# Building the expert gate matrix: one float32 matmul per token against three bfloat16 ones on one-hots made four tokens at a time

## The chip, the cores and the metric

The kernel runs on one core of one Trainium2 chip. The metric is the device time of the whole program in microseconds (us), median of three runs. TensorE (PE) multiplies, VectorE (DVE) and ScalarE (ACT) do elementwise work, GpSimd (POOL) one subtraction that is repeated, and SyncE (SP) issues the transfers.

## The reference

The program is one layer of a decoder trunk over 512 tokens of width 1024: a combined input projection, two attention mixers, and then a feed-forward of retrieved single-neuron experts. The change is in this last part alone, in float32:

```python
def peer_ffn(xn, w_query, sub_keys, u, v):          # per block of 128 tokens
    q = (xb @ w_query).reshape(BLOCK, PEER_HEADS, 2, PEER_HALF)
    s = jnp.einsum('thcd,hckd->thck', q, sub_keys)
    s1, i1 = lax.top_k(s[:, :, 0], PEER_TOPK)       # 16 of 128 keys, twice, in 8 heads
    s2, i2 = lax.top_k(s[:, :, 1], PEER_TOPK)
    cand_s = s1[..., :, None] + s2[..., None, :]
    cand_i = i1[..., :, None] * N_KEYS + i2[..., None, :]
    ...
    top_s, top_c = lax.top_k(cand_s, PEER_TOPK)     # 16 experts (i, j) of 128 x 128 per head
    g = jax.nn.softmax(top_s, axis=-1)
    act = jax.nn.gelu(jnp.einsum('thkd,td->thk', ue, xb), approximate=False)
    return jnp.einsum('thk,thkd->td', g * act, ve)
```

## The kernel before

Nothing is gathered. The kernel computes the hidden activation of all 16,384 experts for all 512 tokens, and multiplies it with a gate matrix that is zero where a token did not pick an expert. `route` makes both, and `experts` then multiplies with `v`.

**The gate matrix.** Each token has 128 picks: a row i, a column j and a weight g. For a tile of 128 tokens they are transposed to `picksT` (`picksT[:, i % 2, 0]` rows, `1` columns, `2` weights; picks on the partitions, tokens along the free axis). For one token `hot_i` is 128 picks x 128 keys with the weight at the pick's row, `hot_j` the same with a one at its column, and `hot_i.T @ hot_j`, a matmul over the 128 picks, is the token's 128 x 128 gate matrix. DVE makes two operations per token in `one_hot`, PE one float32 matmul per token in `gates`, ACT copies a bank of four tokens out of PSUM into `stage` (128 rows x 128 columns x 128 tokens), and SP stores `stage` once a tile is whole.

**The order.** Four tokens are a group (`HOT`), eight groups a turn, four turns a tile (`TURNS`), four tiles in all. There are two group buffers and two PSUM banks (6 and 7): DVE fills buffer b after PE's matmuls of two groups before (`hot_used`), PE starts a group after DVE's last operation on it (`hot_ready`) and ACT's copy of two groups before (`gate_out`).

**Columns.** The hidden activations come in 128 columns (`column`), each 24 matmuls of 512 tokens in three split products (L1299 to L1301). Behind each, ACT runs the Gelu (`act_w`, L1364) and rounds the next `u` (`uh`, L1357), POOL subtracts to get its low part (`ul`, L1434), and SP loads the one after. Per tile PE runs ten pairs of columns alone (`ahead`, `bridge`), and then four pairs mixed with the gates (`turns`): after every second group half a column, 12 matmuls. I call two groups and the half column behind them a step; a tile has 16 steps, and a whole column ends with every second one. DVE picks the experts of the next tile (`chosen`) once it is through with the one-hots of a tile.

Of the kernel before, what the change touches and what calls it, by code (L numbers as in the profile page):

```python
# [21 lines left out]
BF16 = mybir.dt.bfloat16  # L22
I32 = mybir.dt.int32
U32 = mybir.dt.uint32
ALU = mybir.AluOpType
# [3 lines left out]
P = 128  # L29
# [20 lines left out]
PEER_TOPK = 16  # L50
N_KEYS = 128
# [97 lines left out]
def bank(m, b, n=1):  # L149
    return m.psum[:, b * 512:(b + n) * 512]  # L150


def placer(nc, start, limit=16481 + 212860):
    at = [start]

    def sb(name, shape, dt=F32):
        size = mybir.dt.size(dt)
        for n in shape[1:]:
            size *= n
        size = -(-size // 32) * 32  # L160
        assert at[0] + size <= limit, (name, at[0] + size - limit)
        t = nc.alloc_sbuf_tensor_at(name, shape, dt, offset=at[0])
        at[0] += size
        return t
    return sb
# [13 lines left out]
def inverse_root(nc, link, out, root, square):  # L179

    link(nc.vector.reciprocal(out, root))
    link(nc.vector.tensor_tensor(root, out, out, ALU.mult))
    link(nc.vector.tensor_tensor(root, root, square, ALU.mult))
    link(nc.vector.tensor_scalar(root, root, -0.5, 1.5, ALU.mult, ALU.add))
    link(nc.vector.tensor_tensor(out, out, root, ALU.mult))
# [919 lines left out]


HOT = 4
TURN_TOKENS = 8 * HOT
TURNS = P // TURN_TOKENS
TURN_GROUPS = TURN_TOKENS // HOT  # L1110
# [12 lines left out]
def route(nc, m, d):  # L1123
    sb = placer(nc, m.free1)
    stage = sb("stage", [P, N_KEYS, P])

    early = placer(nc, m.free1, m.free1 + 4 * N_KEYS * P)
    wq = early("wq", [P, DC, D])
# [18 lines left out]
    top = sb("top", [P, PEER_HEADS, PEER_TOPK])  # L1147
    top_at = sb("top_at", [P, PEER_HEADS, PEER_TOPK], U32)
    top_at_f = sb("top_at_f", [P, PEER_HEADS, PEER_TOPK])
    hits = sb("hits", [P, HIT_HEADS, PEER_TOPK, CANDS])  # L1150
    pick = sb("pick", [P, PEER_HEADS, PEER_TOPK])
    pick_i = sb("pick_i", [P, 3, PICKS], I32)
    picks = sb("picks", [P, 3, PICKS])
    norm = sb("norm", [P, PEER_HEADS])
    picksT = sb("picksT", [P, 2, 3, P])
    hot_i = sb("hot_i", [P, 2, HOT, N_KEYS])
    hot_j = sb("hot_j", [P, 2, HOT, N_KEYS])

    wq_loaded = [nc.alloc_semaphore(f"wq_loaded{k}") for k in range(2)]
    names = ("keys_loaded ms_ready_c root_ready_c hn_ready hn_turned hnT_ready queried q_out q_turned "  # L1160
             "qT_ready routed s_out s_read shifted exped picks_ready picks_turned picksT_ready "
             "x_split hot_ready hot_used gate_out stage_stored u_high u_low hidden activated dve_order_c").split()
    s = {n: nc.alloc_semaphore(n) for n in names}
    u_loaded = [nc.alloc_semaphore(f"u_loaded{k}") for k in range(2)]
    act_stored = [nc.alloc_semaphore(f"act_stored{k}") for k in range(2)]
# [28 lines left out]
    with nc.Block() as block:  # L1194
# [51 lines left out]
        def _(pe):  # L1246
# [62 lines left out]
            def gates(i):  # L1309

                def body(t, pair):
                    for g in range(TURN_GROUPS):
                        b = g % 2
                        n = t * TURN_GROUPS + (i * TURNS * TURN_GROUPS + g + 1)
                        pe.wait_ge(s["hot_ready"], n)
                        pe.wait_ge(s["gate_out"], n)
                        for q in range(HOT):
                            last_mm = nc.tensor.matmul(bank(m, 6 + b)[:, q * P:(q + 1) * P], hot_i[:, b, q],  # L1318
                                                       hot_j[:, b, q], start=True, stop=True, skip_group_check=True)
                        last_mm.then_inc(s["hot_used"], 1)  # L1320
                        if b == 1:

                            k = g // COLUMN_GROUPS
                            at = g % COLUMN_GROUPS + 1
                            column(pair * 2 + k, k, False, (at - 2) * DC // COLUMN_GROUPS, at * DC // COLUMN_GROUPS)
                turns(pe, i, body)
# [122 lines left out]
        def _(dve):  # L1449
            link = chain(dve, s["dve_order_c"])  # L1450

            def normed(i):

                if i >= 2:
                    dve.wait_ge(s["hn_turned"], i - 1)
                nc.vector.tensor_scalar(hn[:, i % 2], m.stream[:, i, :], inv[:, i:i + 1], None,
                                        ALU.mult).then_inc(s["hn_ready"], 1)
# [73 lines left out]

            def one_hot(i):
                dve.wait_ge(s["picksT_ready"], i + 1)

                def body(t, pair):
                    for g in range(TURN_GROUPS):
                        b = g % 2
                        dve.wait_ge(s["hot_used"], t * TURN_GROUPS + (i * TURNS * TURN_GROUPS + g + 1))
                        for q in range(HOT):
                            tok = t * TURN_TOKENS + (g * HOT + q)  # L1540
                            nc.vector.tensor_scalar(hot_i[:, b, q], m.iota[:], picksT[:, i % 2, 0, bass.ds(tok, 1)],  # L1541
                                                    picksT[:, i % 2, 2, bass.ds(tok, 1)], ALU.is_equal, ALU.mult)
                            last_hot = nc.vector.tensor_scalar(hot_j[:, b, q], m.iota[:],  # L1543
                                                               picksT[:, i % 2, 1, bass.ds(tok, 1)], None, ALU.is_equal)
                        last_hot.then_inc(s["hot_ready"], 1)
                turns(dve, i, body)

            nc.vector.tensor_scalar(ms[:], m.stream_sums[:], 1.0 / D, EPS, ALU.mult, ALU.add).then_inc(s["ms_ready_c"], 1)
            dve.wait_ge(s["root_ready_c"], 1)
            inverse_root(nc, link, inv[:], root[:], ms[:])  # L1550
            normed(0)
            for i in range(NT):
                if i + 1 < NT:
# [223 lines left out]
```

## Time and profile before

| | |
|---|---|
| median of 3 runs | 2352.19 us (2349.07 to 2356.54) |
| profiled execution, first to last instruction | 2344.2 us |
| PE busy in it | 2162.8 us (92%) |
| DVE busy in it | 1218.6 us (52%) |
| ACT busy in it | 748.8 us (32%) |
| POOL busy in it | 409.4 us (17%) |
| mean granted TensorE clock | 0.971 of full |

The profiled execution's own time is given as its span of 2344.2 us; it lies 8.0 us below the median of the runs, which count what stands around the instructions too. Times in the rows are microseconds from the span's start. A matmul's duration in the trace contains its latency, so consecutive ones overlap; what one costs is read from start to start. A float32 matmul of this kernel with 128 columns shows as two records, and each matmul has a weight load (PEld) of its own.

### The profile page before, as it was taken

To read this page: it belongs to the slowest core of one execution; us is meant where nothing else is said; L and a number is where in the kernel's file an instruction comes from. 1 tells how busy PE (TensorE), PEld (TensorE's weight loads), DVE (VectorE), ACT (ScalarE), POOL (GpSimd) and SP (SyncE) were. 2 spreads that over 40 slices of the span, in tenths; PEclk is the share of its full clock that TensorE was granted. 3 is DMA by queue.
4 is the path that set the end of the run, shared out by engine and by line. 5 is a ranking of instruction groups with operands and counts; after the bars stand their busy time and mean duration, and the time that the engine had idled before them with its cause. 6 is when DMAs were issued, how large, how long until landed. Compare 5 with 4: busy or idle time off the path is not lost.

```text
span 2344.2 us, 29842 instructions
## 1 busy us (share of the span) xinstructions
PE 2162.8 (92%) x9791; PEld 1700.9 (73%) x9794; DVE 1218.6 (52%) x3132; ACT 748.8 (32%) x1099; POOL 409.4 (17%) x160
## 2 busy tenths in 40 slices
PE   6799978889899989998998998897999999999998
PEld 5678755554347877777777777776888888888887
DVE  7852569732217289538917963810544444444443
ACT  3322234320013344245234423532322222222221
POOL 3233300000003422432342243232000000000000
PEclk9999969889899999999999999999999999999999
DMA  3122120000203423632662363156655554555542
GB/s 104 69 73 95 49 108 1 37 1 1 98 19 108 148 68 130 224 126 80 205 199 76 121 229 130 67 193 237 218 208 183 194 200 180 205 188 188 205 179 107
DMA packets 164892, 307.63 MB, mean 131 GB/s; under 512 B 9808, under 2 KB 77008, under 8 KB 162016
## 3 DMA queue, kind: packets, MB, share of 16 engines
q1 hardware_dynamic: 164656, 306.81, 37.6%
q8 instruction: 31, 0.51, 0.1%
q14 instruction: 29, 0.24, 0.0%
q10 hardware_dynamic: 176, 0.07, 0.0%
HBM read 237.64 MB, written 69.21 MB: 131 GB/s over the span
## 4 chain that ended last, share of the span: by engine, by line
PE 56%; DVE 5%; DMA 4%; issue 3%; DVEq 2%; POOL 2%; ACT 2%; SPq 1%; POOLq 0%; ACTq 0%
PE psum L1627 30%; PE psum L1299 7%; PE psum L1301 7%; PE psum L1300 7%; DMA u<-in_u 3%; PE psum L1318 3%; PE psum L1265 2%; DVE hot_j L1543 2%; DVE hot_i L1541 2%; POOL ul L1434 2%; ACT uh L1357 1%; DVEq L1541 1%; ACT act_w L1364 1%; DVEq L1543 0%; DMA wq<-in_w_query 0%
## 5 line engine op out<-in xcount | busy, mean ns | idle before, releaser
L1434 POOL TENSOR_TENSOR ul<-u,uh 128x1024 fp32r<-128x1024 f32 x128 | 315.1, 2462 | 1023.5 <-ACT uh L1357 1023.5
L1299 PE MATMUL psum<-xh,uh 128*128 128x512 f32 x1024 | 408.5, 399 | 11.9 <-POOL ul L1434 9.1
L1301 PE MATMUL psum<-xh,ul 128*128 128x512 f32 x1024 | 400.1, 391 | 0.0
L1300 PE MATMUL psum<-xl,uh 128*128 128x512 f32 x1024 | 399.9, 391 | 0.0
L1661 DVE TENSOR_TENSOR vl<-v,vh 128x1024 fp32r<-128x1024 f32 x128 | 156.8, 1225 | 367.1 <-ACT vh L1645 367.1
L1627 PE MATMUL psum<-vh,wh 128*128 128x512 f32 x1024 | 316.0, 390 | 11.3 <-DVE wl L1664 11.3
L1627 PE MATMUL psum<-vl,wh 128*128 128x512 f32 x1024 | 315.7, 389 | 0.0
L1627 PE MATMUL psum<-vh,wl 128*128 128x512 f32 x1024 | 315.7, 389 | 0.0
L1645 ACT CAST vh<-v 128x1024 fp32r<-128x1024 f32 x128 | 135.0, 1055 | 485.1 <-PE psum L1627 472.9
L1541 DVE TENSOR_SCALAR hot_i<-iota,picksT 128x128 f32<-128x128 f32 x512 | 208.8, 408 | 84.0 <-PE psum L1318 47.9
L1299 PEld LDWEIGHTS psum<-xh,uh 128*128 128x128 f32 x1024 | 193.5, 189 | 59.2 <-issue 11.6
L1627 PEld LDWEIGHTS psum<-vh,wh 128*128 128x128 f32 x1024 | 192.6, 188 | 51.6 <-DVE vl L1661 11.7
L1301 PEld LDWEIGHTS psum<-xh,ul 128*128 128x128 f32 x1024 | 192.9, 188 | 41.4
L1627 PEld LDWEIGHTS psum<-vh,wl 128*128 128x128 f32 x1024 | 192.5, 188 | 40.1
L1627 PEld LDWEIGHTS psum<-vl,wh 128*128 128x128 f32 x1024 | 192.5, 188 | 40.1
L1300 PEld LDWEIGHTS psum<-xl,uh 128*128 128x128 f32 x1024 | 193.3, 189 | 37.3
L1364 ACT ACTIVATE act_w<-psum 128x512 f32<-128x512 f32 x128 | 76.5, 598 | 392.9 <-PE psum L1301 392.9
L1318 PE MATMUL psum<-hot_j,hot_i 128*128 128x128 f32 x1024 | 139.4, 285 | 48.8 <-DVE hot_j L1543 48.8
L1318 PEld LDWEIGHTS psum<-hot_j,hot_i 128*128 128x128 f32 x1024 | 126.8, 195 | 69.9 <-DVE hot_j L1543 67.3
L1398 ACT COPY stage<-psum 128x512 f32 x128 | 132.9, 1092 | 129.7 <-PE psum L1318 129.7
L1543 DVE TENSOR_SCALAR hot_j<-iota,picksT 128x128 f32<-128x128 f32 x512 | 168.7, 329 | 0.0
L1357 ACT CAST uh<-u 128x1024 fp32r<-128x1024 f32 x128 | 133.4, 1042 | 54.3 <-DMA u<-in_u 54.2
(244 smaller groups left out, 2518.3 us busy)
## 6 DMA issues: line engine op xcount, KB each, us to landing
u<-in_u SPq DMA_DIRECT2D x128, 512.0 KB, 3.6
v<-in_v SPq DMA_DIRECT2D x63, 1024.0 KB, 4.9
act_mat<-act_w SPq DMA_DIRECT2D x128, 256.0 KB, 2.1
gate_mat<-stage SPq DMA_DIRECT2D x32, 1024.0 KB, 4.6
gate<-gate_mat SPq DMA_DIRECT2D x63, 512.0 KB, 5.6
act_v<-act_mat SPq DMA_DIRECT2D x63, 512.0 KB, 6.4
wraw<-in_w_wide SPq DMA_DIRECT2D x18, 1024.0 KB, 5.2
w_out<-in_w_out SPq DMA_DIRECT2D x1, 4096.0 KB, 17.0
```

The source lines that it names most:

```text
L1299: nc.tensor.matmul(bank(m, 4 + k), uh[:, k, c], m.xh[:, c], start=(c == 0), stop=False)
L1300: nc.tensor.matmul(bank(m, 4 + k), uh[:, k, c], m.xl[:, c], start=False, stop=False)
L1301: last = nc.tensor.matmul(bank(m, 4 + k), ul[:, k, c], m.xh[:, c], start=False, stop=(c == DC - 1))
L1318: last_mm = nc.tensor.matmul(bank(m, 6 + b)[:, q * P:(q + 1) * P], hot_i[:, b, q], hot_j[:, b, q], start=True, stop=True, skip_group_check ...
L1357: nc.scalar.copy(uh[:, k], u[:, k]).then_inc(s["u_high"], 1)
L1398: nc.scalar.copy(stage[:, :, bass.ds(at, HOT)].rearrange("p j t -> p t j"), bank(m, 6 + b).rearrange("p (t j) -> p t j", t=HOT)).then_inc( ...
L1434: nc.gpsimd.tensor_tensor(ul[:, k], u[:, k], uh[:, k].bitcast(F32), ALU.subtract).then_inc(s["u_low"], 1)
L1541: nc.vector.tensor_scalar(hot_i[:, b, q], m.iota[:], picksT[:, i % 2, 0, bass.ds(tok, 1)], picksT[:, i % 2, 2, bass.ds(tok, 1)], ALU.is_eq ...
L1543: last_hot = nc.vector.tensor_scalar(hot_j[:, b, q], m.iota[:], picksT[:, i % 2, 1, bass.ds(tok, 1)], None, ALU.is_equal)
L1627: mm = nc.tensor.matmul(bank(m, 2 * i + half), lhs[:, k, tok], rhs[:, k, half * 512:(half + 1) * 512], start=first and k == 0 and p == 0, ...
L1645: nc.scalar.copy(vh[:, k], v[:, k]).then_inc(s["v_high"], 1)
L1661: nc.vector.tensor_tensor(vl[:, k], v[:, k], vh[:, k].bitcast(F32), ALU.subtract).then_inc(s["v_low"], 1)
```

## The change

The keys' numbers are laid out once as `keys_b`, bfloat16, each number four times side by side. Per tile DVE rounds rows and columns to bfloat16 (`places_b`, exact for numbers to 127) and splits the weight into three bfloat16 parts that add up to it (`weight_b`, with `rest` between them). Per group it then runs five two-input operations on 512 bfloat16 elements each: a comparison for `hot_j`, one for `hot_i`, and three products of `hot_j` with a weight part, `hot_w`. Within a buffer the token is now the innermost index, so that the matmuls read keys with a step of four elements. PE runs three bfloat16 matmuls per token into the same place, `hot_i` against each of the three parts. A semaphore `hot_cols` makes the products wait for `hot_j`. `hits`, `places_b` and `rest` are placed on the same memory; nothing else moves.

```diff
 HOT = 4
+PARTS = 3
...
+    hits = sb("hits", [P, HIT_HEADS, PEER_TOPK, CANDS])
+    beside_hits = placer(nc, m.free1 + 4 * N_KEYS * P)
+    places_b = beside_hits("places_b", [P, 2, P], BF16)
+    rest = beside_hits("rest", [P, P])
...
-    hot_i = sb("hot_i", [P, 2, HOT, N_KEYS])
-    hot_j = sb("hot_j", [P, 2, HOT, N_KEYS])
+    keys_b = sb("keys_b", [P, N_KEYS, HOT], BF16)
+    weight_b = sb("weight_b", [P, PARTS, P], BF16)
+    hot_i = sb("hot_i", [P, 2, N_KEYS, HOT], BF16)
+    hot_j = sb("hot_j", [P, 2, N_KEYS, HOT], BF16)
+    hot_w = sb("hot_w", [P, 2, PARTS, N_KEYS, HOT], BF16)
...
                         for q in range(HOT):
-                            last_mm = nc.tensor.matmul(bank(m, 6 + b)[:, q * P:(q + 1) * P], hot_i[:, b, q],
-                                                       hot_j[:, b, q], start=True, stop=True, skip_group_check=True)
+                            for k in range(PARTS):
+                                last_mm = nc.tensor.matmul(bank(m, 6 + b)[:, q * P:(q + 1) * P], hot_i[:, b, :, q],
+                                                           hot_w[:, b, k, :, q], start=(k == 0), stop=(k == PARTS - 1),
+                                                           skip_group_check=True)
...
             def one_hot(i):
                 dve.wait_ge(s["picksT_ready"], i + 1)
+                weight = picksT[:, i % 2, 2]
+                nc.vector.tensor_copy(places_b[:], picksT[:, i % 2, 0:2])
+                link(nc.vector.tensor_copy(weight_b[:, 0], weight))
+                link(nc.vector.tensor_tensor(rest[:], weight, weight_b[:, 0], ALU.subtract))
+                link(nc.vector.tensor_copy(weight_b[:, 1], rest[:]))
+                link(nc.vector.tensor_tensor(rest[:], rest[:], weight_b[:, 1], ALU.subtract))
+                link(nc.vector.tensor_copy(weight_b[:, 2], rest[:]))
...
-                        for q in range(HOT):
-                            tok = t * TURN_TOKENS + (g * HOT + q)
-                            nc.vector.tensor_scalar(hot_i[:, b, q], m.iota[:], picksT[:, i % 2, 0, bass.ds(tok, 1)],
-                                                    picksT[:, i % 2, 2, bass.ds(tok, 1)], ALU.is_equal, ALU.mult)
-                            last_hot = nc.vector.tensor_scalar(hot_j[:, b, q], m.iota[:],
-                                                               picksT[:, i % 2, 1, bass.ds(tok, 1)], None, ALU.is_equal)
+                        some = bass.ds(t * TURN_TOKENS + g * HOT, HOT)
+                        row, col = (bcast(places_b[:, k, some], 1, N_KEYS) for k in range(2))
+                        nc.vector.tensor_tensor(hot_j[:, b], keys_b[:], col, ALU.is_equal).then_inc(s["hot_cols"], 1)
+                        nc.vector.tensor_tensor(hot_i[:, b], keys_b[:], row, ALU.is_equal)
+                        dve.wait_ge(s["hot_cols"], t * TURN_GROUPS + (i * TURNS * TURN_GROUPS + g + 1))
+                        for k in range(PARTS):
+                            last_hot = nc.vector.tensor_tensor(hot_w[:, b, k], hot_j[:, b],
+                                                               bcast(weight_b[:, k, some], 1, N_KEYS), ALU.mult)
                         last_hot.then_inc(s["hot_ready"], 1)
...
             inverse_root(nc, link, inv[:], root[:], ms[:])
+            nc.vector.tensor_copy(keys_b[:], bcast(m.iota[:], 2, HOT))
             normed(0)
```

On DVE the first group of a tile stands so before, in the queue behind the picks of that tile (L1541 makes `hot_i`, L1543 `hot_j`; the pairs go on to the fourth token):

```order
L1541 ISA [waits hot_used]
L1541 TENSOR_SCALAR hot_i<-iota,picksT 128x128
L1543 ISA
L1543 TENSOR_SCALAR hot_j<-iota,picksT 128x128
L1541 ISA
L1541 TENSOR_SCALAR hot_i<-iota,picksT 128x128
```

After the change the same place holds the tile's splitting and then one group:

```order
L1544 CAST places_b<-picksT 128x256 [waits picksT_ready]
L1545 CAST weight_b<-picksT 128x128
L1546 TENSOR_TENSOR rest<-picksT,weight_b 128x128 [waits dve_order_c]
L1547 CAST weight_b<-rest 128x128 [waits dve_order_c]
L1548 TENSOR_TENSOR rest<-rest,weight_b 128x128 [waits dve_order_c]
L1549 CAST weight_b<-rest 128x128 [waits dve_order_c]
...
L1557 TENSOR_TENSOR hot_j<-keys_b,places_b 128x512
L1558 ISA
L1558 TENSOR_TENSOR hot_i<-keys_b,places_b 128x512
L1561 REGISTER_ALU [waits hot_cols]
L1561 TENSOR_TENSOR hot_w<-hot_j,weight_b 128x512
```

Eight operations of 128 elements became five of 512, with six new ones ahead of a tile's first group.

On PE one step of the gates stands so before (the half column's 12 matmuls follow):

```order
L1318 MATMUL psum<-hot_j,hot_i 128x128 [waits gate_out,hot_ready]
L1318 MATMUL psum<-hot_j,hot_i 128x128 x3
L1315 REGISTER_ALU
L1318 MATMUL psum<-hot_j,hot_i 128x128 [waits gate_out,hot_ready]
L1318 MATMUL psum<-hot_j,hot_i 128x128 x3
```

And after the change:

```order
L1326 MATMUL psum<-hot_w,hot_i 128x128 [waits gate_out,hot_ready]
L1326 MATMUL psum<-hot_w,hot_i 128x128 x11
L1322 REGISTER_ALU
L1326 MATMUL psum<-hot_w,hot_i 128x128 [waits gate_out,hot_ready]
L1326 MATMUL psum<-hot_w,hot_i 128x128 x11
```

The waits stand where they stood; a group has 12 bfloat16 matmuls in place of 4 float32 ones (8 records).

## Rows read from the trace of the kernel before

**Rows 1.** The chain that ended last, shares of the span by engine

```profile
PE 56%; DVE 5%; DMA 4%; issue 3%; DVEq 2%; POOL 2%; ACT 2%; SPq 1%; POOLq 0%; ACTq 0%
```

**Rows 2.** Window, length, busy of PE, PEld, DVE, ACT, POOL (instructions); clock, DMA, GB/s

```profile
825.36:911.20 85.84, 74.40 (x429) 62.87 (x428) 73.59 (x257) 43.44 (x46) 17.16 (x8) 0.98 0.20 67
...
861.32:872.24 10.92, 9.65 (x59) 8.13 (x58) 9.42 (x32) 5.71 (x8) 2.45 (x1) 1.00 0.22 72
```

**Rows 3.** PE in order of time: start, us, what, idle before it

```profile
871.48 1.95 PE L1318 MATMUL psum<-hot_j,hot_i 128*128 128x128 f32 x16
873.18 0.48 PE L1299 MATMUL psum<-xh,uh 128*128 128x512 f32 x1
...
876.83 1.16 PE L1318 MATMUL psum<-hot_j,hot_i 128*128 128x128 f32 x8 [0.67 <-DVE hot_j L1543]
878.64 1.16 PE L1318 MATMUL psum<-hot_j,hot_i 128*128 128x128 f32 x8 [0.65 <-DVE hot_j L1543]
879.56 0.47 PE L1299 MATMUL psum<-xh,uh 128*128 128x512 f32 x1
...
882.41 1.95 PE L1318 MATMUL psum<-hot_j,hot_i 128*128 128x128 f32 x16
```

**Rows 4.** DVE in order of time, same cycle

```profile
872.73 0.35 DVE L1541 TENSOR_SCALAR hot_i<-iota,picksT 128x128 f32<-128x128 f32 x1 [1.45 <-PE psum L1318]
...
873.45 2.43 DVE L1543 TENSOR_SCALAR hot_j<-iota,picksT 128x128 f32<-128x128 f32 x1
875.80 0.33 DVE L1541 TENSOR_SCALAR hot_i<-iota,picksT 128x128 f32<-128x128 f32 x1
```

**Rows 5.** POOL in order of time, same cycle

```profile
873.37 2.43 POOL L1434 TENSOR_TENSOR ul<-u,uh 128x1024 fp32r<-128x1024 f32 x1 [8.24 <-ACT uh L1357]
```

**Rows 6.** DVE in order of time while it picks experts

```profile
942.25 0.29 DVE L1511 TENSOR_TENSOR top<-top,norm 128x128 f32<-128x128 f32 x1
942.46 1.82 DVE L1514 TENSOR_TENSOR hits<-top_at_f,iota 128x1600 f32<-128x1600 f32 x1
...
948.02 2.72 DVE L1514 TENSOR_TENSOR hits<-top_at_f,iota 128x1600 f32<-128x1600 f32 x1
```

**Rows 7.** POOL in order of time beside it

```profile
946.66 2.39 POOL L1434 TENSOR_TENSOR ul<-u,uh 128x1024 fp32r<-128x1024 f32 x1 [4.74 <-ACT uh L1357]
```

**Rows 8.** Groups by line and shape: count, busy us, mean ns of one

```profile
L1664 DVE TENSOR_TENSOR wl<-gate,wh 128x512 fp32r<-128x512 f32 x128 | 87.5, 684 | 0.0
```

**Rows 9.** PE and its weight loads beside the first bfloat16 matmuls

```profile
299.57 0.22 PE L785 MATMUL psum<-tri_b,ident_b 128*128 128x128 bf16 x1
299.62 0.46 PE L775 MATMUL psum<-akT,aqT 128*128 128x144 f32 x2
```

**Rows 10.** Weight loads of two lines: shortest, median, longest ns

```profile
L785 PEld LDWEIGHTS psum<-tri_b,ident_b x40: 95/98/292, 299.4 to 447.7; 128*128 128x128 bf16 x40
L1318 PEld LDWEIGHTS psum<-hot_j,hot_i x1024: 186/192/333, 827.1 to 1532.8; 128*128 128x128 f32 x171
```

**Rows 11.** PE at the first gates of the first tile

```profile
827.15 1.16 PE L1318 MATMUL psum<-hot_j,hot_i 128*128 128x128 f32 x8 [1.78 <-DVE hot_j L1543]
828.96 2.07 PE L1318 MATMUL psum<-hot_j,hot_i 128*128 128x128 f32 x8 [0.65 <-DVE hot_j L1543]
830.68 0.77 PE L1299 MATMUL psum<-xh,uh 128*128 128x512 f32 x1
```

**Rows 12.** DVE in order of time, small operations linked by semaphores, and a long wait

```profile
930.49 0.30 DVE L1502 CAST idx_f<-idx 128x256 f32<-128x256 uint32 x1
930.82 0.23 DVE L1504 TENSOR_SCALAR idx_f<-idx_f 128x128 f32<-128x128 f32 x1
...
813.81 0.29 DVE L1527 TENSOR_REDUCE norm<-top 128x8 f32<-128x128 f32 x1 [40.84 <-ACT top L1418]
```

**Rows 13.** DVE and PE at the start of the query projection

```profile
633.44 0.69 DVE L1467 CAST xh<-hnT 128x1024 fp32r<-128x1024 f32 x1
...
637.00 2.05 PE L1265 MATMUL psum<-wq,hnT 128*128 128x512 f32 x2 [4.86 <-DMA wq<-in_w_query]
```

More of the change, by code:

```diff
@@ L1149, in route @@
     top_at_f = sb("top_at_f", [P, PEER_HEADS, PEER_TOPK])
-    hits = sb("hits", [P, HIT_HEADS, PEER_TOPK, CANDS])
     pick = sb("pick", [P, PEER_HEADS, PEER_TOPK])
@@ L1161, in route @@
              "qT_ready routed s_out s_read shifted exped picks_ready picks_turned picksT_ready "
-             "x_split hot_ready hot_used gate_out stage_stored u_high u_low hidden activated dve_order_c").split()
+             "x_split hot_cols hot_ready hot_used gate_out stage_stored u_high u_low hidden activated dve_order_c").split()
     s = {n: nc.alloc_semaphore(n) for n in names}
```

## The prediction

> **What bounds the kernel now.** I read the chain that ended last first: more than half of the span is PE work [rows 1], so only what makes PE wait or do more counts. The change touches the four stretches of gates, so I went on to the busy times by stretch. The first stretch lasts 85.8 us, with PE busy for 74.4 of them and DVE for 73.6 [rows 2]. Neither is full, and the same holds inside one steady cycle of two steps, 10.92 us with PE busy 9.65 and DVE 9.42 [rows 2]. Two engines that are both busy to some 87% wait for each other in turns, and the order of time of one cycle shows where.
>
> PE runs two groups back to back, 16 records in 1.70 us (871.48 to 873.18), a half column until it waits at about 876.2, a group at 876.83, the next at 878.64, and from 879.56 a half column until 882.41, where the same starts again: 10.93 us [rows 3]. DVE has finished both its buffers before 871.48 and sits idle for 1.45 us; it restarts at 872.73, 0.40 after PE's first group ends (871.48 + 0.85 = 872.33) [rows 3, 4]. Its third operation then takes 2.43 us instead of about 0.28 [rows 4], exactly as long as POOL's subtraction, 873.37 to 875.80 [rows 5]. So PE gets its next group late. Written as a sum, with G a group on PE, H a group on DVE, S what POOL costs DVE, C a half column:
>
> cycle = G (0.85) + restart (0.40) + 2 H + S + hand-over (0.12) + G (0.92) + C (2.85) = 10.93.
>
> H is 1.81, the distance of PE's two waiting groups (876.83 to 878.64) [rows 3]. S is 2.15: one operation occupied DVE for 2.35 (873.45 to 875.80) instead of 0.20. The sum is 0.85 + 0.40 + 3.62 + 2.15 + 0.12 + 0.92 + 2.85 = 10.91, which leaves 0.02. The second step of a cycle is PE's alone: 0.92 + 2.85 = 3.77 against DVE's 2 H + 0.12 = 3.74. Each tile has 7 such cycles (16 steps less a first without the POOL wait and the even one at the end), 28 in all.
>
> **DVE's group.** Eight one-input operations leave, five two-input ones of 512 bfloat16 elements come. No row shows such an operation. In float32 a two-input operation of 128 elements is followed after 0.21 us, and one of 1600 lasts 1.53 longer than one of 128 (1.82 against 0.29) [rows 6], so 1.04 ns per element and 0.077 fixed. At that rate 512 elements cost 0.53 + 0.08 = 0.61, in agreement with a duration of 684 ns for this very shape [rows 8], and a group costs 5 x 0.61 = 3.05. That is the upper bound. DVE does move two elements at once where the operand paths allow: a one-input conversion of 1024 elements took 0.69 [rows 13], where the two-input rate would make it 0.29 + 896 x 1.04 ns = 1.22. Two 2-byte elements are as wide as one float32, so I take half the time per element: 0.27 + 0.08 = 0.34, H = 1.72; with a fixed part of 0.06 instead of 0.08 it would be 1.64, and I take 1.72. The wait on `hot_cols` costs nothing by this: `hot_j` is over 0.42 after its start (0.27 and the 0.15 by which 684 ns exceeds 0.53), when `hot_i` still runs until 0.69. Without that cover it would cost about 0.1 per group. Thus 2 H changes by 2 x (1.72 - 1.81) = -0.18.
>
> The Trainium skill, "VectorE: DVE Perf Modes", The perf-mode tier table, has tensor_tensor in bfloat16 at twice the float32 rate; the page leads to the same 1.72, and no row here tests it.
>
> **POOL's hold.** Does a two-input operation still wait for POOL? The rows say so for float32: the comparison at 948.02 took 2.72 where others take 1.82 (the 942.46 one), its start falling into POOL's 946.66 to 949.05 and its end 1.69 behind POOL's [rows 6, 7]. So S stays. Bounds: 2.15 as now, or 2.4 if POOL first lets a longer operation end and DVE then waits out all of it; I take 2.25, +0.10.
>
> The Trainium skill, "SBUF — State Buffer", on the shared port pair, says that a Vector instruction with two SBUF inputs contends with a GpSimd one that reads SBUF; the trace agrees (2.72 against 1.82).
>
> **PE's group.** 8 float32 records of 0.106 us (1.70 / 16) [rows 3] give way to 12 bfloat16 matmuls with 12 loads. The one bfloat16 matmul of 128 columns with a neighbour starts 0.05 before it [rows 9], and a bfloat16 load is recorded with 98 ns against 192 [rows 10]. If nothing gets shorter, it stays 0.106. So a group is 0.60 to 1.28; I take 0.062 each, 0.74, near the low end because load and matmul both show half, and above it because twelve short pairs follow each other. Both G's together: -0.22.
>
> The step of four elements is new and has no row. The Trainium skill, "SBUF — State Buffer", on SBUF cachelines, wants two hits per 16-byte line for full rate; a step of 8 bytes gives just two, so by the page nothing is lost. "TensorE: Matmul & The Clock Gate", Back-to-back issue gap, gives about 81 ns per matmul in a stream of 128-column pairs: 0.97 a group, estimated from that page.
>
> **Once per tile.** Six small operations stand ahead of the first group: linked ones follow after their duration and 0.03 (930.49 + 0.30, next at 930.82) [rows 12], so 0.19 + 3 x (0.23 + 0.03) + 2 x (0.29 + 0.03) = 1.6 us, bare on the path, since PE waits 1.78 there already [rows 11]. The first group saves 0.09, and three groups outside the cycles save 0.11 each on PE: +1.2 per tile, +4.8. PE's idle time grows from 1.8 to 3.3 us. After today's the granted clock fell from 2.4 to 1.2 GHz in the first tile (the second group took 2.07 instead of 1.16, the first wide matmul 0.77 instead of 0.47 [rows 11, 3]), some 0.8 + 0.8 us. I count one such fall more, +1.5, and keep 0 and 5 for the range.
>
> **At nothing.** `keys_b` is one conversion ahead of `normed(0)`; `hnT` is there at 633.4, when its conversion starts, and PE waits for weights until 637.00 [rows 13], which covers 3.6 us. Without that cover it would cost 0.7 at most. What DVE does for the next tile starts when the one-hots end, and it waits 40.8 us for the tile's end [rows 12]. ACT's copies and SP's stores are unchanged, behind nothing new; the POOL operation may start up to 0.3 later, and its result is used a cycle later.
>
> **Sum.** Cycle -0.18 + 0.10 - 0.22 = -0.30, x 28 = -8.4; tiles +4.8; clock +1.5. Together -2.1 against the profiled span of 2344.2, that is 2342. The median of runs lies 8.0 above the span; I carry that over: 2350.
>
> **Rivals.**
> *PE's pairs don't get shorter* (a strided read or the load sets 0.106): G = 1.28, cycle -0.18 + 0.10 + 0.86 = +0.78, x 28 = +22; twelve groups outside +5; first steps 6.4 - 0.4; clock +1.5: 2387. At 0.081 a matmul it is +13, 2365. It decides from 0.070 on, where the gain per cycle is gone. For it: twelve loads instead of eight, never seen in a row. Against it: 98 ns and 0.05. Chance 0.22. By the page's 81 ns this rival is the outcome, at its lower number.
> *DVE's operations don't overlap*: each costs its whole 0.42, H = 2.1: cycle +0.48, +13, with the tiles +21: 2373. Against it: 0.21 after an operation of 0.29. Chance 0.08.
> *DVE gains no rate*: H = 3.05; DVE then works without pause, 32 x 3.05 + 7 x 2.25 + 1.6 = 115 us per tile against 85.5: +118, 2470. Chance 0.05.
> *Both new kinds are as short as the bounds*: H = 1.64, G = 0.62, S as now: cycle -0.80, -22, with tiles and clock -18: 2334; half of it 2341. Chance 0.23.
> *Packed two-input operations don't wait for POOL*: the cycle becomes PE's alone, 4 x 0.74 + 2 x 2.85 = 8.7: -2.2 x 28 = -63, +6: 2295. Against it rows 6 and 7. Chance 0.05.
> *My forecast, nearly nothing*: 2344 to 2359. Chance 0.37.
>
> **Numbers.** A difference under 0.3% (7 us) can't be told from none. Faster: 0.23 + 0.05 = 0.28. Same: 0.37. Slower: 0.22 + 0.08 + 0.05 = 0.35. The predicted time is the forecast's, 2350. The range takes in the short ends and PE's long one, 2330 to 2387, and leaves out 0.05 + 0.05 and a few tails.
>
> **What would show it.** `hot_w` operations 0.34 apart and one per cycle stretched to about 2.7; twelve matmuls in 0.74; PE's wait ahead of the third group nearly as now; a cycle of 10.6; the first group of a tile 1.5 later. The forecast is wrong if PE's twelve take over 0.84, if `hot_w` is 0.6 apart, or if no DVE operation is stretched beside POOL.

## The result, and the profile after

The kernel after the change takes 2389.04 us (2386.04 to 2396.2, four runs), the one before 2350.63 (2347.78 to 2356.54, four runs). The ratio is 1.0152 with a 95% interval of 1.012 to 1.0184: slower by 38 us. The forecast was 2350, the range ended at 2387.

Three lines of the page of the changed kernel: busy time of the engines, and the shares of the chain that ended last, by engine and by line, which answer to [rows 1].

```profile
PE 2234.1 (94%) x10303; PEld 1755.9 (74%) x10306; DVE 1204.1 (50%) x2773; ACT 756.3 (32%) x1099; POOL 416.1 (17%) x160
...
PE 58%; DVE 4%; DMA 4%; issue 3%; POOL 2%; ACT 1%; SPq 1%; DVEq 0%; POOLq 0%; ACTq 0%
PE psum L1646 29%; PE psum L1306 7%; PE psum L1308 7%; PE psum L1307 7%; PE psum L1326 6%; DMA u<-in_u 3%; PE psum L1272 2%; DVE hot_w L1561 2%; POOL ul L1443 2%; ACT uh L1366 1%; DVE hot_j L1557 0%; ACT act_w L1373 0%; DMA wq<-in_w_query 0
```

PE has 71 us more of busy time than before the change, DVE 14 less. The gate matmul L1326 alone is 6% of the chain.

The windows of the first stretch of gates and of one steady cycle, same columns as [rows 2]:

```profile
838.18:927.73 89.55, 88.58 (x554) 74.39 (x555) 69.08 (x157) 43.12 (x45) 17.79 (x7) 0.98 0.18 62
873.58:885.17 11.59, 11.50 (x73) 9.63 (x73) 9.10 (x20) 5.81 (x6) 2.68 (x1) 1.00 0.19 68
```

Here PE is full: 88.58 of 89.55, and 11.50 of the 11.59 of a cycle, at the full granted clock. A cycle took 10.93 before.

PE in order of time in that cycle, to be laid beside [rows 3]:

```profile
873.58 2.99 PE L1326 MATMUL psum<-hot_w,hot_i 128*128 128x128 bf16 x24
876.32 0.48 PE L1306 MATMUL psum<-xh,uh 128*128 128x512 f32 x1
...
879.34 3.26 PE L1326 MATMUL psum<-hot_w,hot_i 128*128 128x128 bf16 x24
882.35 0.48 PE L1306 MATMUL psum<-xh,uh 128*128 128x512 f32 x1
...
885.17 1.11 PE L1326 MATMUL psum<-hot_w,hot_i 128*128 128x128 bf16 x8
```

From the first gate matmul to the first wide one behind them it is 876.32 - 873.58 = 2.74 us for 24: 0.114 each, 1.37 a group. The forecast had 0.062 and 0.74, the kernel before 0.85.

DVE and then POOL in the same cycle [rows 4, 5]:

```profile
875.30 0.43 DVE L1557 TENSOR_TENSOR hot_j<-keys_b,places_b 128x512 bf16<-128x512 bf16 x1 [2.38 <-PE psum L1326]
875.65 0.42 DVE L1558 TENSOR_TENSOR hot_i<-keys_b,places_b 128x512 bf16<-128x512 bf16 x1
875.98 3.30 DVE L1561 TENSOR_TENSOR hot_w<-hot_j,weight_b 128x512 bf16<-128x512 bf16 x3
879.20 0.41 DVE L1557 TENSOR_TENSOR hot_j<-keys_b,places_b 128x512 bf16<-128x512 bf16 x1
879.53 0.41 DVE L1558 TENSOR_TENSOR hot_i<-keys_b,places_b 128x512 bf16<-128x512 bf16 x1
879.87 1.09 DVE L1561 TENSOR_TENSOR hot_w<-hot_j,weight_b 128x512 bf16<-128x512 bf16 x3
881.09 0.43 DVE L1557 TENSOR_TENSOR hot_j<-keys_b,places_b 128x512 bf16<-128x512 bf16 x1
```

```profile
875.64 2.68 POOL L1443 TENSOR_TENSOR ul<-u,uh 128x1024 fp32r<-128x1024 f32 x1 [9.24 <-ACT uh L1366]
```

Operations of a group start 0.33 to 0.35 apart and a group takes 1.67. Three products last 3.30 beside POOL and 1.09 without it, so POOL costs DVE 2.21. DVE now waits 2.38 for PE where it waited 1.45.

With these the sum of the prediction closes: cycle = G 1.37 + restart 0.35 (874.95 to 875.30) + 2 H 3.35 + S 2.21 + hand-over 0.12 + G 1.37 + C 2.82 = 11.59, and the trace has 11.59. PE's work alone would be 4 x 1.37 + 2 x 2.85 = 11.18: the two limits lie 0.4 apart, and PE still waits 0.17 and 0.27 in a cycle.

The weight load and the matmul of the gates, durations in ns as shortest, median, longest (for the loads, [rows 10]):

```profile
L1326 PEld LDWEIGHTS psum<-hot_w,hot_i x1536: 112/117/141, 838.2 to 1573.7; 128*128 128x128 bf16 x192
L1326 PE MATMUL psum<-hot_w,hot_i x1536: 282/297/304, 838.2 to 1573.8; 128*128 128x128 bf16 x192
```

The load is short, near the 98 ns of the bfloat16 loads of before. The matmul is not: its median is 297 ns, where the float32 records of the kernel before (L1318) had 275 and its bfloat16 matmuls (L785) 219.

The start of the first tile [rows 11]. DVE in order of time:

```profile
832.53 2.16 DVE L1544 CAST places_b<-picksT 128x256 bf16<-128x256 f32 x1 [8.59 <-ACT picksT L1430]
...
835.78 0.23 DVE L1549 CAST weight_b<-rest 128x128 bf16<-128x128 f32 x1
836.36 0.43 DVE L1557 TENSOR_TENSOR hot_j<-keys_b,places_b 128x512 bf16<-128x512 bf16 x1 [0.35 <-DVE weight_b L1549]
```

And PE there:

```profile
838.18 3.26 PE L1326 MATMUL psum<-hot_w,hot_i 128*128 128x128 bf16 x24 [3.73 <-DVE hot_w L1561]
841.19 0.77 PE L1306 MATMUL psum<-xh,uh 128*128 128x512 f32 x1
```

PE waits 3.73 where it waited 1.78, so the splitting costs 1.95 per tile.

**Where the 40.8 us of span went** (2385.0 against 2344.2), by the starts of the first and the last gate matmul of each tile in both traces. The four stretches between them grew from 85.0, 83.4, 85.0 and 85.3 to 90.6, 91.0, 91.2 and 90.7, by 24.7 together; 28 cycles of 0.66 more and twelve groups of 0.52 more give just that. The three stretches from one tile's last gate to the next tile's first grew by 5.2, which is the splitting. Behind the last gate nothing changed (-0.1). The first gate came 11.0 later (838.2 against 827.2), and only 1.95 of that is the splitting. 7.6 come from ahead of the changed code: `w_out`'s first matmul starts at 542.4 instead of 534.8, and in the attention stage from 300 to 400 us the granted clock was 0.69 in this profile and 0.78 in that of before. This varies from profile to profile with the same instructions (0.78 and 535.8 in the first experiment, 0.69 and 542.1 in the fourth). The rest, some 1.5, is a fall of the granted clock in the columns ahead of the first gates, which are unchanged too (0.57 from 716 to 720 us in this profile, 1.00 in those of before and of the fourth experiment). So I compare kernels by a **gate window** as well, from the first gate matmul's start to the last one's, which is free of both: 705.7 before, 735.6 after, +29.9.

### The profile page after: what moved, and what is told of

Read it like the earlier page. It is cut to its first block, busy times and chain, and to the rows that moved or that the text cites. A ratio compares the mean times of both kernels' runs of the same rounds, so it can differ in the third digit from the quotient of the medians.

```text
span 2385.0 us, 30115 instructions
## 1 busy us (share of the span) xinstructions
PE 2234.1 (94%) x10303; PEld 1755.9 (74%) x10306; DVE 1204.1 (50%) x2773; ACT 756.3 (32%) x1099; POOL 416.1 (17%) x160
## 4 chain that ended last, share of the span: by engine, by line
PE 58%; DVE 4%; DMA 4%; issue 3%; POOL 2%; ACT 1%; SPq 1%; DVEq 0%; POOLq 0%; ACTq 0%
PE psum L1646 29%; PE psum L1306 7%; PE psum L1308 7%; PE psum L1307 7%; PE psum L1326 6%; DMA u<-in_u 3%; PE psum L1272 2%; DVE hot_w L1561 2%; POOL ul L1443 2%; ACT uh L1366 1%; DVE hot_j L1557 0%; ACT act_w L1373 0%; DMA wq<-in_w_query 0%; DVE places_b L1544 0%; SPq L1227 0%
## 5 line engine op out<-in xcount | busy, mean ns | idle before, releaser
L1443 POOL TENSOR_TENSOR ul<-u,uh 128x1024 fp32r<-128x1024 f32 x128 | 321.6, 2513 | 1057.4 <-ACT uh L1366 1057.4
L1326 PE MATMUL psum<-hot_w,hot_i 128*128 128x128 bf16 x1536 | 197.4, 297 | 22.2 <-DVE hot_w L1561 18.4
L1326 PEld LDWEIGHTS psum<-hot_w,hot_i 128*128 128x128 bf16 x1536 | 167.4, 118 | 54.5 <-DVE hot_w L1561 44.0
L1407 ACT COPY stage<-psum 128x512 f32 x128 | 139.3, 1088 | 155.2 <-PE psum L1326 155.2
L1561 DVE TENSOR_TENSOR hot_w<-hot_j,weight_b 128x512 bf16<-128x512 bf16 x384 | 145.8, 434 | 0.0
L592 PE MATMUL psum<-whi,xTh 128*128 128x512 f32 (+1 forms) x344 | 137.5, 400 | 4.7 <-DVE xTl L350 3.1
```

What stands on the lines that cost most here:

```text
L592: nc.tensor.matmul(ps, xh, wh, start=(part == 0 and k == 0), stop=False)
L1407: nc.scalar.copy(stage[:, :, bass.ds(at, HOT)].rearrange("p j t -> p t j"), bank(m, 6 + b).rearrange("p (t j) -> p t j", t=HOT)).then_inc( ...
L1443: nc.gpsimd.tensor_tensor(ul[:, k], u[:, k], uh[:, k].bitcast(F32), ALU.subtract).then_inc(s["u_low"], 1)
L1561: last_hot = nc.vector.tensor_tensor(hot_w[:, b, k], hot_j[:, b], bcast(weight_b[:, k, some], 1, N_KEYS), ALU.mult)
```

## The experiments

The question was which part of the twelve pairs costs 0.114: the step of four elements in the weights, the step in the moving operand, or the pair itself.

**1. Both operands without a step.**

```diff
-  matmul(..., hot_i[:, b, :, q], hot_w[:, b, k, :, q], ...)
+  matmul(..., hot_i[:, b, q * 32:(q + 1) * 32].rearrange("p j t -> p (j t)"),
+              hot_w[:, b, k, q * 32:(q + 1) * 32].rearrange("p j t -> p (j t)"), ...)
```

> The changed kernel, but each gate matmul reads 128 neighbouring elements (a quarter of the group's buffer) as weights and as moving operand, in place of every fourth: the gates' values are thus not the token's; counts, sizes and DVE's work are the same. The changed kernel's 24 matmuls take 2.74 us (0.114 each) and its cycle 11.6 us. Theory A (the step of four elements is what the 12 matmuls pay for): about 0.06 each, G near 0.75, the cycle falls to DVE's, about 10.6, and the time to about 2355. Theory B (any bfloat16 pair of load and matmul of 128 columns costs 0.11 here): G stays 1.37, cycle 11.6, time 2389 unchanged.

Measured: 2338.31 us (2334.2 to 2340.5) against 2356.51 of the kernel before on the same chip, ratio 0.9925 (0.9895 to 0.9954). Gate window 690.0. PE in order of time:

```profile
871.01 0.84 PE L1326 MATMUL psum<-hot_w,hot_i 128*128 128x128 bf16 x12 [0.83 <-DVE hot_w L1561]
874.50 1.51 PE L1326 MATMUL psum<-hot_w,hot_i 128*128 128x128 bf16 x24
...
881.20 0.84 PE L1326 MATMUL psum<-hot_w,hot_i 128*128 128x128 bf16 x12 [0.83 <-DVE hot_w L1561]
```

The 24 take 1.33 to the wide matmul at 875.83: 0.055 each, and the cycle is 10.19. The pair is not slow; the step is.

**2 and 3. One operand without a step**: the moving one (`hot_w`) alone, and the weights (`hot_i`) alone, by the same edit.

> As the run with both dense, but only the moving operand is read without a step (values of the gates are again not the token's). If the moving operand's step of 8 bytes is the cost: 0.06 each as with both dense, and the matmul's recorded duration falls from 297 ns towards 220. If it is the weights' step: 0.114 stays and loads stay at 117 ns.

> As the run with both dense, but only the weights are read without a step (values of the gates are not the token's). If the weights' step is the cost: 0.06 each and loads of 98 ns. If it is the moving operand's: 0.114 and 297 ns stay, only the load's record falls to 98 ns.

Measured: 2342.77 us and gate window 693.3 with the moving operand dense, 2390.51 us and 732.0 with the weights dense (one run each). The matmul records of the two kernels, first the moving operand dense:

```profile
L1326 PE MATMUL psum<-hot_w,hot_i x1536: 219/219/311, 836.0 to 1529.3; 128*128 128x128 bf16 x192
```

And the weights dense:

```profile
L1326 PE MATMUL psum<-hot_w,hot_i x1536: 273/294/299, 842.2 to 1574.2; 128*128 128x128 bf16 x192
```

The loss comes from the step in the moving operand. The step in the weights lengthens the load's record from 98 to 113 ns (medians of experiments 1 and 2) and costs little: with dense weights the 24 matmuls take 1.32 instead of 1.34 (experiment 1 against 2) and 2.69 instead of 2.75 (experiment 3 against the changed kernel), medians over all double groups at the full clock. That is 1 to 2 ns a matmul and 3 to 4 us of gate window in each pair.

**4. A step of two elements**: two tokens side by side instead of four. The cut shows one buffer of three; `hot_i`, `hot_j` and the operands of DVE's operations change in the same way.

```diff
-    keys_b = sb("keys_b", [P, N_KEYS, HOT], BF16)
-    hot_w = sb("hot_w", [P, 2, PARTS, N_KEYS, HOT], BF16)
+    keys_b = sb("keys_b", [P, N_KEYS, 2], BF16)
+    hot_w = sb("hot_w", [P, 2, PARTS, 2, N_KEYS, 2], BF16)
...
-  matmul(..., hot_i[:, b, :, q], hot_w[:, b, k, :, q], ...)
+  matmul(..., hot_i[:, b, q // 2, :, q % 2], hot_w[:, b, k, q // 2, :, q % 2], ...)
```

> The changed kernel with two tokens side by side in place of four (step of 4 bytes for both operands), the same five DVE operations of 512 elements over two pairs. Theory A with a cost that grows with the step (four or more hits per 16-byte line are free): 0.06 each, cycle 10.6, time about 2355. Theory A with a cost for any step: 0.114 and 2389 stay. Theory B: 0.114 and 2389 stay too. DVE's operations should stay 0.34 apart; if rows of two elements cost it the double rate, 0.6 apart and a time over 2450.

Measured: 2342.29 us (2337.8 to 2350.27, ten runs) against the same 2356.51, ratio 0.9953 (0.9935 to 0.9971). Gate window 691.4. PE in order of time:

```profile
868.23 1.56 PE L1326 MATMUL psum<-hot_w,hot_i 128*128 128x128 bf16 x24
869.60 0.47 PE L1306 MATMUL psum<-xh,uh 128*128 128x512 f32 x1
...
873.27 0.86 PE L1326 MATMUL psum<-hot_w,hot_i 128*128 128x128 bf16 x12 [0.67 <-DVE hot_w L1565]
874.95 0.86 PE L1326 MATMUL psum<-hot_w,hot_i 128*128 128x128 bf16 x12 [0.81 <-DVE hot_w L1565]
875.62 0.47 PE L1306 MATMUL psum<-xh,uh 128*128 128x512 f32 x1
...
878.47 1.56 PE L1326 MATMUL psum<-hot_w,hot_i 128*128 128x128 bf16 x24
```

1.37 us for 24 is 0.057 each, as good as dense, and PE waits for DVE again. DVE's operations stay 0.335 apart, so the shorter row of two costs DVE nothing. The cycle is 10.24: the prediction's sum with G = 0.68 is 0.68 + 0.34 + 5.56 (2 H + S) + 0.14 + 0.67 + 2.85 = 10.24. This version keeps the three parts and the five operations of the change and is faster than the kernel before, by 0.5%.

**5 and 6. Steps of three and of eight elements** in the moving operand, to see by what law it slows down.

```diff
-  hot_w[:, b, k, :, q]
+  hot_w[:, b, k].rearrange("p j t -> p (j t)")[:, q:q + 128 * 3:3]                # experiment 5
+  hot_w[:, b].rearrange("p k j t -> p (k j t)")[:, q + 4 * k:q + 4 * k + 1024:8]  # experiment 6
```

> The changed kernel with a moving operand read with a step of three elements (6 bytes) in place of four; the values of the gates are not the token's. So far: 0.057 us a matmul at steps of one and two elements, 0.114 at four. Theory L (each new 16-byte line costs the same, 64 lines in about 0.107 us at step four, so 1.67 ns a line): 48 lines, about 0.08 each, G about 1.0. Theory T (below four hits in a line the read halves, whatever the number): 0.114 as with step four, G 1.37.

> As with step three, but a step of eight elements (16 bytes), a new line for every column; the values of the gates are not the token's. Theory L: 128 lines, 0.21 each, G about 2.6, PE alone sets the cycle at 4 x 2.6 + 5.7 = 16 us and the time rises by 28 x 4.5 and the groups outside, to over 2520. Theory T: 0.114, the changed kernel's 2389.

Measured: 2358.86 us with three (gate window 715.1), 2671.31 with eight (1012.2), one run each. PE with step three, then with step eight:

```profile
872.48 2.33 PE L1326 MATMUL psum<-hot_w,hot_i 128*128 128x128 bf16 x24
874.59 0.48 PE L1306 MATMUL psum<-xh,uh 128*128 128x512 f32 x1
```

```profile
861.82 5.70 PE L1326 MATMUL psum<-hot_w,hot_i 128*128 128x128 bf16 x24
867.16 0.79 PE L1306 MATMUL psum<-xh,uh 128*128 128x512 f32 x1
867.74 0.63 PE L1307 MATMUL psum<-xl,uh 128*128 128x512 f32 x1
868.17 0.63 PE L1308 MATMUL psum<-xh,ul 128*128 128x512 f32 x1
```

| step, elements | 1 | 2 | 3 | 4 | 8 |
|---|---|---|---|---|---|
| us for 24 matmuls | 1.33 | 1.37 | 2.11 | 2.74 | 5.34 |
| ns each | 55 | 57 | 88 | 114 | 222 |

The columns of the table are one double group each, at steps 1 to 4 at the full granted clock. From two elements (4 bytes) on the time is proportional to the step, 28 to 29 ns per matmul and element of step; at one element it is hardly shorter than at two. Counted in 16-byte lines, as in the expectations, 128 elements touch 48, 64 and 128 at steps three, four and eight, and it is 1.8, 1.8 and 1.7 ns a line. The runs show the proportion to the step, not that lines are its cause.

What the traces add is that the array's clock does not set this time. The granted clock falls to its lower level, half the full one, at the start of most tiles' gates in these profiles. Twelve matmuls take 0.65 at the full level and 1.22 at the lower one with both operands dense, but 1.34 and 1.33 with a step of four in the moving operand (medians over the groups that lie wholly at one level), and the 24 of step eight take 5.33 and 5.35.

Step eight lost more than the matmuls themselves, and the expectation missed that. The wide matmuls behind the gates start 0.43 apart there instead of 0.23, at the lower level (0.50 granted from 867.16 to 871.16), and a step took 10.24 us, of which 5.34 are gates and 4.9 the half column. From 872 to 882 us the granted clock is 0.66 on average. PE was not idle ahead of that fall: it had run a half column and then, from 861.82 to 864.77 and still at 1.00, only slow-reading matmuls. Why the clock fell I did not test further; at step four it stays at 0.98 over the first stretch.

**7 and 8. POOL's subtraction cut to an eighth**, in the changed kernel and in that of step two (`ul` then comes from 128 of its 1024 elements, and the matmuls read these again and again).

```diff
-  last = nc.tensor.matmul(bank(m, 4 + k), ul[:, k, c], m.xh[:, c], ...)
+  last = nc.tensor.matmul(bank(m, 4 + k), ul[:, k, 0], m.xh[:, c], ...)
...
-  nc.gpsimd.tensor_tensor(ul[:, k], u[:, k], uh[:, k].bitcast(F32), ALU.subtract)
+  nc.gpsimd.tensor_tensor(ul[:, k, 0], u[:, k, 0], uh[:, k, 0].bitcast(F32), ALU.subtract)
```

> The changed kernel with POOL subtracting one eighth (128 of 1024 elements), and the low part's matmuls all reading that eighth: part of the hidden activations is thus not computed. PE's counts and sizes stay. If in the changed kernel PE's twelve matmuls set the cycle and POOL's hold on DVE is almost covered, the cycle goes from 11.59 to 4 x 1.37 + 2 x 2.85 = 11.2, and the time to about 2378. If DVE's stall still set it, the cycle would lose 2.2 and the time would go to about 2330.

> The kernel with two tokens side by side (cycle 10.24 us) with the same short subtraction on POOL (part of the hidden activations not computed). If POOL's hold on DVE is what PE waits for there, the cycle falls to PE's own 4 x 0.685 + 2 x 2.85 = 8.4 to 8.6, and the time by about 28 x 1.7, to 2295. If two-input operations of bfloat16 were not held by POOL, nothing changes from 2342.

Measured: 2349.97 us (window 700.7) and 2261.78 us (618.7), one run each. PE of the changed kernel without the hold:

```profile
868.22 3.01 PE L1326 MATMUL psum<-hot_w,hot_i 128*128 128x128 bf16 x24
873.80 3.01 PE L1326 MATMUL psum<-hot_w,hot_i 128*128 128x128 bf16 x24
879.38 0.88 PE L1326 MATMUL psum<-hot_w,hot_i 128*128 128x128 bf16 x6
```

The cycle is 11.16, PE's work alone (11.18), 0.43 less than after the change: with G = 1.37 the hold hides nearly all behind PE. With step two the cycle falls from 10.24 to 8.43. So the hold decides where PE is short, and bfloat16 two-input operations do wait for POOL. The gate window of experiment 7 fell by more than the 12 us of 28 cycles: by 34.9, of which the four stretches give 15.8 and the three between them 19.1. There columns run alone and wait for this subtraction at their start: against an even distance of 0.228 the starts of the wide matmuls there lie 14.0 us too far apart in sum in the changed kernel, and 0.5 here. The other 5.5 are the wait ahead of a tile's first gate, which falls by 1.7 to 1.9 each time (3.72 to 1.85 in the third tile), as DVE's first operation no longer falls beside a long subtraction. I had counted neither, and the expectations, about 2378 and 2295, were 28 and 33 too high.

**9 to 12. More buffers, fewer parts.** In experiments 1, 4 and 5 the group's chain PE - DVE - POOL - PE sets the cycle because DVE may be only two groups ahead. Experiment 9 gives the kernel of step two four group buffers (with `hot_j` and `hits` placed on memory that is free at the time), experiment 11 the same to the kernel before; 10 takes one of the three weight parts out of that of step two, so that the weight is less exact, and 12 does 9 and 10 together. The first cut is experiment 9 against the changed kernel, the second the line of experiment 10.

```diff
-    hot_i = sb("hot_i", [P, 2, N_KEYS, HOT], BF16)
+    hot_i = sb("hot_i", [P, 4, 2, N_KEYS, 2], BF16)
...
-            pe.sem_inc(s["hot_used"], 2)
+            pe.sem_inc(s["hot_used"], 4)
...
-                        b = g % 2
+                        b = g % 4
```
```diff
-PARTS = 3
+PARTS = 2
```

> Two tokens side by side, and four group buffers in place of two, so that DVE runs up to four groups ahead (PSUM still has two banks for them). The cycle was 10.24 us because DVE restarts only when PE's first group is over, and then meets POOL. Without that wait DVE's own work sets it: 4 x 1.67 + 2.2 = 8.9 us, PE's is 8.4: -1.3 x 28, about 2305. If the wait is not the two buffers' but the PSUM banks' or ACT's copies', it stays at 10.2 and 2342.

> Two tokens side by side, with two bfloat16 parts of the weight in place of three (the weight keeps about 16 bits): one DVE operation and four matmuls less per group. By the sum of the prediction, cycle = G + 0.35 + 2 H + S + 0.13 + G + C with G = 0.46, H = 1.34, S = 2.2, C = 2.85: 9.1 us in place of 10.24, about 2311. If only PE's part counted, it would be 9.8 and about 2330.

> The kernel before with four group buffers in place of two, all else as before. If the wait of DVE for a free buffer and then for POOL is what made its cycle 10.93, DVE's own work sets it now: 4 x 1.81 + 2.15 = 9.4 us, PE's is 9.2: -1.5 x 28, about 2310 against 2351. If bfloat16 and two tokens side by side are needed for a gain, it stays at 2351.

> The kernel of step two with both further edits: four group buffers instead of two, and two parts of the weight instead of three (the weight is then exact to some 16 bits, not 24; this is what the kernel leaves out). Theory P (two buffers were what let POOL's hold reach PE, and with four the busier of PE and DVE sets the pace): PE needs per cycle 4 x 0.46 + 2 x 2.85 = 7.54 us (8 matmuls of 0.057 per group), DVE 4 x 1.34 + 2.2 = 7.56, so a cycle of about 7.6 to 7.8 where the four buffers with three parts had 8.4 to 9.8, and about 2265 to 2275 in all. Theory Q (behind the buffers stands a second limit, POOL's subtraction ul, which the run with four buffers and three parts showed PE waiting for once in some cycles, since each ul follows a chain over ACT and the load of u of about 9 to 10 us per column): the cycle stays at 8.4 or over, PE's waits are on ul, and the time is 2295 or over.

| | us | ratio to the kernel before (95%) | gate window |
|---|---|---|---|
| 9, step two, four buffers | 2303.41 (2295.96 to 2304.81) | 0.9773 (0.9743 to 0.9804) | 653.5 |
| 10, step two, two parts | 2307.36 (2304.04 to 2312.84) | 0.9806 (0.9779 to 0.9834) | 652.1 |
| 11, before, four buffers | 2309.67 (2300.91 to 2312.32) | 0.9796 (0.9765 to 0.9827) | 657.4 |
| 12, step two, both | 2261.51 (2257.56 to 2265.26) | 0.9622 (0.9591 to 0.9652) | 607.6 |

The kernel before took 2353.71 us beside 9 to 11 and 2352.88 beside 12. Experiment 11 shows that two buffers bound the kernel before as well: PE's double groups follow each other at 864.37, 868.89, 873.41, 878.15, 882.67, 887.49, a cycle of 9.04 to 9.34 instead of 10.93. Against it the bfloat16 form of experiment 9 brings nothing that can be told apart, since the intervals overlap. Experiment 10 has a cycle of 9.11 (865.60 to 874.71), one product less in each of two groups and four matmuls less in each of two: 10.24 - 2 x 0.335 - 2 x 0.23 = 9.11.

Experiment 9 met a wait that I had not priced. PE, DVE and POOL in order of time:

```profile
874.26 1.55 PE L1325 MATMUL psum<-hot_w,hot_i 128*128 128x128 bf16 x24
877.02 0.49 PE L1305 MATMUL psum<-xh,uh 128*128 128x512 f32 x1 [1.21 <-POOL ul L1442]
```

```profile
873.58 1.08 DVE L1564 TENSOR_TENSOR hot_w<-hot_j,weight_b 128x512 bf16<-128x512 bf16 x3
875.27 1.91 DVE L1560 TENSOR_TENSOR hot_j<-keys_b,places_b 128x512 bf16<-128x512 bf16 x1 [0.61 <-PE psum L1325]
877.10 2.62 DVE L1561 TENSOR_TENSOR hot_i<-keys_b,places_b 128x512 bf16<-128x512 bf16 x1
```

```profile
867.89 11.54 POOL L1442 TENSOR_TENSOR ul<-u,uh 128x1024 fp32r<-128x1024 f32 x2 [3.24 <-ACT uh L1365]
```

From 864.86 to 874.66 DVE runs one two-input operation after another, and none of them is stretched; POOL, ready at 867.89, gets through only once DVE pauses, and two of its operations take 11.54 us instead of about 5. Then PE waits for `ul`. In the whole run PE waited 20.6 us for `ul` (7.6 after the change).

It takes more than a DVE without pauses. In experiment 11 DVE works just as much without one, on the one-input float32 comparisons, and POOL is not held up. The same stretch of the experiments 9 and 11, columns as in [rows 2]:

```profile
848.00:900.00 52.00, 50.79 (x434) 42.31 (x433) 50.20 (x121) 32.91 (x36) 30.16 (x6) 1.00 0.28 91
848.00:900.00 52.00, 51.86 (x317) 45.83 (x316) 52.00 (x179) 32.10 (x36) 13.33 (x6) 1.00 0.24 81
```

In experiment 11 DVE is busy for all 52.00 us, and all 28 subtractions beside gates take 2.40 to 2.58; in experiment 9 they take up to 9.4. The one that POOL starts at 894.40 ends at 903.64, 2.32 after DVE went over from its last two-input product to a one-input search (L1486, at 901.32), without a pause. So it is the unbroken row of two-input bfloat16 operations that keeps POOL out; there the hold works both ways. PE's waits for `ul` are 20.6 us in experiment 9 and 10.3 in experiment 11.

In experiment 12 DVE has less to do and pauses in each cycle. PE and POOL there:

```profile
862.27 1.10 PE L1325 MATMUL psum<-hot_w,hot_i 128*128 128x128 bf16 x16
...
866.01 1.10 PE L1325 MATMUL psum<-hot_w,hot_i 128*128 128x128 bf16 x16
...
869.75 1.10 PE L1325 MATMUL psum<-hot_w,hot_i 128*128 128x128 bf16 x16
```

```profile
864.33 3.95 POOL L1442 TENSOR_TENSOR ul<-u,uh 128x1024 fp32r<-128x1024 f32 x1 [3.62 <-ACT uh L1365]
871.63 4.21 POOL L1442 TENSOR_TENSOR ul<-u,uh 128x1024 fp32r<-128x1024 f32 x1 [3.35 <-ACT uh L1365]
```

The cycle is 7.48, PE's work alone, and POOL's 4 us no longer set PE's steps (9.5 us of waits on `ul` in all). The reading that POOL's subtraction would keep the cycle over 8.4 fell. This is the fastest version, with a weight of two parts; the fastest with all three is experiment 9.

## Why the prediction was wrong

**PE's group, the step that failed.** "I take 0.062 each, 0.74": it measured 0.114 and 1.37, beyond my upper bound of 1.28, for which nothing was to get shorter. The forecast's own words have the gap: "The step of four elements is new and has no row". I took it at nothing, as the rule I cited had it, instead of giving it a bound from below and above. The Trainium skill, "SBUF — State Buffer", on SBUF cachelines, has two hits per 16-byte line suffice; the measurement differs for the moving operand (114 ns with two hits, 57 with four), and it decides. In the weights the step costs 1 to 2 ns a matmul (experiments 1 to 3). The price I took for the pair itself was right: 0.055 to 0.057 in experiments 1 and 4. The rival's mark "it decides from 0.070 on" lies between what was run: 0.057 gave a gain, and 0.088 (experiment 5) a loss by the gate window (715.1 against 705.7), with 2358.86 against 2354.67 in single runs. By the prediction's own terms the gain per cycle is gone at 0.074 (-0.18 + 0.10 + 2 x 0.04), not at 0.070. The Trainium skill, "TensorE: Matmul & The Clock Gate", Back-to-back issue gap, with 81 ns, fits neither form.

**The cycle's sum held.** It gives 11.59 after the change and 10.24 with step two once G is the measured one. G enters twice, with 1.55 for both in the forecast (today's 0.85 and 0.92 less 0.22) and 2.74 in the trace, +1.19. H took back 0.09 of it, restart 0.05, S 0.04 and C 0.03; 0.02 is left. Against the forecast of 10.63 that is +0.96, times 28 cycles 27 us of the miss.

**DVE's group** was 1.72 in the forecast and 1.67 in the trace. Half the time per element is right: 0.335 from start to start for 512 elements. The wait on `hot_cols` shows nowhere.

**POOL's hold**: 2.25 against 2.21. The rival "packed two-input operations don't wait for POOL" is out; experiment 8 shows what it would have been worth.

**Once per tile**: 1.6 bare on PE's path against 1.95; the first operation fell beside POOL and took 2.16, and the first comparison waited 0.35 for the last part. Over the first 5 us of the four tiles' gates the granted clock was 0.66, 0.50, 0.51 and 0.51, against 0.68, 1.00, 0.78 and 0.50 before: one fall more, in the second tile, as forecast, after PE's wait of 3.7 us. But the 24.7 us by which the stretches grew leave nothing for it, so the 1.5 that I counted show nowhere. Twelve groups outside the cycles cost 12 x 0.63 = 7.6 against the forecast.

**At nothing**: `keys_b` shows no wait. The matmuls of the query projection came 7.8 later than before and `w_out`'s 7.6, which leaves at most 0.2.

**The sum of the miss**: 27 for the cycles, 7.6 for the groups outside, 1.4 for four tile starts, 7.6 for the attention stage's clock and 1.5 for the clock's fall at 716 us, less the 1.5 counted for the clock at the gates, take the predicted span of 2342 to 2385.6; it measured 2385.0. I also carried 8.0 from the span to the median. A run's own time is only 1.8 above its span (2386.79 against 2385.0); the other 6 of before were the distance of the median run from the profiled one, which was no property of the kernel. After the change the median lay 4.0 above the span, so that term was 4 too large and hid as much of the miss.

**The rival that came true** was "PE's pairs don't get shorter", at 2387, by a strided read, as its parenthesis says. Its sign, size and place were right, and its chance of 0.22 was too low for something that no row had shown. That its total lies 2 us from the measured median is in part luck: its G was 0.09 too small and yet its cycle grew by 0.78 where 0.66 was measured, and some 9 us of the profile's growth lie in unchanged code.

## What to carry to other kernels

When a layout puts several items side by side for one engine, look at the step it leaves for the other: TensorE read a bfloat16 moving operand at full rate up to a step of two elements and in proportion slower beyond, while a step of four in the weights cost 1 to 2 ns a matmul, and side by side in twos was as good for VectorE as in fours. Before making operations cheaper, write down the chain of a cycle with its hand-overs; here two more buffers in the old kernel gained 2%, four times what the cheaper operations gained with the step put right. When two engines hold each other up, ask of each kind of operation which of the two it lets through. A new access pattern without a row gets both bounds in the range, above all where its cost enters the chain twice.

## What the runs showed of the hardware

- A strided bfloat16 moving operand costs 28 to 29 ns per 128 columns and element of step (88, 114 and 222 ns at steps 3, 4 and 8), against 55 and 57 at steps 1 and 2. A step of four in the weights adds 15 ns to the load's record and 1 to 2 ns to the pair.
- The time of the strided matmuls is the same at both levels of the granted clock (twelve at step four 1.34 and 1.33 us, dense ones 0.65 and 1.22).
- Twelve pairs of bfloat16 load and matmul follow each other every 55 to 57 ns at the full granted clock.
- The hold between DVE and POOL works in both directions for two-input bfloat16 operations: one beside a subtraction lasts up to 2.2 us longer, and an unbroken row of them stretched two subtractions of POOL to 11.54 us. An unbroken row of one-input float32 comparisons left every subtraction at 2.40 to 2.58 us (experiment 11), though one of them is stretched to about 2.5 each time.
- With step eight in the gates the granted clock was 0.66 on average over a step although PE had work all the time, and the wide matmuls at the lower level started 0.43 apart instead of 0.23.
